# A pre-norm's per-token scale behind the projection, in a two-layer hybrid decoder trunk on one core

## The reference, cut to what matters

```
x = x + rms_post(Mix(rms_pre(x)))
x = x + rms_post2(ConvFFN(rms_pre2(x)))

def rms_norm(x, w):
    y = x * rsqrt(mean(x * x, axis=-1, keepdims=True) + EPS)
    return y * w
```

## Time and profile before

| | us |
|---|---|
| median of 3 runs | 2903.79 (2901.67 to 2905.25) |
| span of the profiled execution, first to last instruction | 2897.5 |
| the profiled execution's own time | not listed; its span is 6.3 below the median |
| TensorE busy in the span | 2551.8 |
| VectorE busy | 1373.6 |
| ScalarE busy | 961.6 |
| POOL busy | 230.7 |

### The profile page before, as it was taken

How to read it: one execution, slowest core, us unless ns; L and a number is a source line. 1 busy time by engine, 2 the same in 40 slices (tenths; PEclk the granted TensorE clock), 3 DMA queues, 4 the chain that set the end, 5 groups by cost and what they waited for, 6 DMA issues and landing times. The chain is left out here.

```text
span 2897.5 us, 41258 instructions
## 1 busy us (share of the span) xinstructions
PE 2551.8 (88%) x16456; PEld 2166.6 (75%) x16456; DVE 1373.6 (47%) x2125; ACT 961.6 (33%) x1396; POOL 230.7 (8%) x350
## 2 busy tenths in 40 slices
PE   6999487998999889999888995879989997999996
PEld 6658333766999879999885782346679997999895
DVE  3338454356333366663342475433563334666623
ACT  3122523332222345553230224332322223454521
POOL 0014132002000000000000132210020000000000
PEclk9999668667999999999999995776779999999998
DMA  3462100221222212222315420012212222222221
GB/s 148 121 192 77 37 1 25 66 66 59 88 88 88 80 52 95 89 95 81 108 59 159 147 73 26 1 42 70 63 62 88 88 80 66 74 95 88 89 88 59
DMA packets 84178, 229.90 MB, mean 79 GB/s; under 512 B 10386, under 2 KB 27794, under 8 KB 83090
## 3 DMA queue, kind: packets, MB, share of 16 engines
q1 hardware_dynamic: 71426, 204.16, 22.0%
q10 hardware_dynamic: 12560, 23.11, 2.5%
HBM read 216.68 MB, written 10.55 MB: 78 GB/s over the span
## 5 line engine op out<-in xcount | busy, mean ns | idle before, releaser
L439 PE MATMUL PS<-XH,WH 128*128 128x260 f32 x3616 | 749.5, 289 | 59.6 <-DVE XL L1195 34.9
L439 PE MATMUL PS<-XL,WH 128*128 128x260 f32 x3616 | 734.5, 285 | 4.1 <-issue 2.7
L439 PE MATMUL PS<-XH,WL 128*128 128x260 f32 x3616 | 733.9, 285 | 0.0
L1219 DVE TENSOR_TENSOR WL<-R,WH 128x1024 fp32r<-128x1024 f32 x240 | 294.3, 1226 | 852.2 <-ACT WH L913 851.8
L913 ACT ACTIVATE WH<-R 128x1024 fp32r<-128x1024 f32 x270 | 285.9, 1059 | 1017.0 <-PE PS L439 860.7
L439 PEld LDWEIGHTS PS<-XH,WH 128*128 128x128 f32 x3616 | 567.5, 191 | 69.7 <-issue 44.8
L439 PEld LDWEIGHTS PS<-XL,WH 128*128 128x128 f32 x3616 | 563.7, 190 | 4.5 <-issue 4.5
L439 PEld LDWEIGHTS PS<-XH,WL 128*128 128x128 f32 x3616 | 563.3, 191 | 0.0
L439 PE MATMUL PS<-FR,WH 128*128 128x260 f32 x1024 | 187.4, 285 | 0.0
L1198 DVE SCALAR_TENSOR_TENSOR S<-S,V 128x510 f32<-128x510 f32 (+1 forms) x176 | 132.1, 751 | 44.9 <-ACT S L1162 41.8
L439 PEld LDWEIGHTS PS<-FR,WH 128*128 128x128 f32 x1024 | 151.0, 190 | 0.1
(11 more groups left out here) (302 smaller groups left out, 3029.8 us busy)
## 6 DMA issues: line engine op xcount, KB each, us to landing
R<-w_up SPq DMA_DIRECT2D x88, 512.0 KB, 3.3
R<-w_gate SPq DMA_DIRECT2D x64, 512.0 KB, 3.3
R<-w_proj SPq DMA_DIRECT2D x58, 512.0 KB, 3.4
R<-v_c SPq DMA_DIRECT2D x128, 192.0 KB, 2.4
R<-w_down SPq DMA_DIRECT2D x44, 512.0 KB, 3.3
R<-k_c SPq DMA_DIRECT2D x72, 256.0 KB, 3.2
R<-k_c ACTq DMA_DIRECT2D x56, 256.0 KB, 3.6
R<-w_br SPq DMA_DIRECT2D x16, 512.0 KB, 3.3
```

The source lines that it names most:

```text
L439: i = mm(PS[:, bank + a, 0:HALF], p[:, w, k * 128:(k + 1) * 128], x[:, a * HALF:(a + 1) * HALF], start=first and p is WH and x is hi, stop ...
L1219: v_.tensor_tensor(WL[:, half(l, m), :], slot(l, SPLIT[m]), WH[:, half(l, m), :].bitcast(f32), ALU.subtract).then_inc(w_lo.sem, 1)
```

## The change

A token's scale RB no longer goes into the projection's input. `XH` and `XL` are now the parts of X x weight alone, and each tile is multiplied by RB when it leaves PSUM: by VectorE for projection tiles 0 to 11, the gates and the up-projection (`proj_out`, `g_raw`, `up_raw`); for projection tiles 12 to 28 ScalarE copies as before and POOL multiplies in place (`scale_projection`). ScalarE's sigmoid and the up-projection's first convolution tap then read the scaled tile from SBUF. The gates' splits of weights run two tiles ahead to the end, so that the out-projection's first two are among them.

Tiles 0 and 1 of each of the four projections behind a pre-norm run together (`first_pair`): per chunk 12 products for both and the sum of the squares. They wait for that chunk's `XL` alone, which VectorE makes between the residual's updates, one chunk behind (`xl_part`); the reciprocal comes after them (`norm_scale`).

At the start the vectors come first, x comes in four pieces of two chunks, the constants in two, with the first two weight tiles in between, and each engine waits for what it uses. y leaves in four pieces, each as soon as its two chunks are updated. The constants' columns are reordered so that the identity, the ones and EPS come first.

```
--- before.py
+++ after.py
...
+        def proj_bank_free(l, c):
+
+            return proj_out.nth(l, c) if c < CUT else proj_raw.nth(l, c - CUT)
...
-            for dst, src in ((X[:, :, :], x_in), (K[:, :], consts), (V[:, :, :], vecs)):
-                sp.dma_start(dst, src).then_inc(loaded.sem, 16)
-            sp.wait_ge(pt_loaded.sem, 16)
+            sp.dma_start(V[:, :, :], vecs).then_inc(v_loaded.sem, 16)
+
+            def load_x(i):
+                sp.dma_start(X[:, 2 * i:2 * i + 2, :], x_in[:, 2 * i:2 * i + 2, :]).then_inc(x_loaded[i].sem, 16)
...
             for l in range(L):
+                if l == 0:
+                    load_x(0)
                 for c in range(CUT):
                     tile(l, proj(c), w_proj[l, c], 1024)
+                    if l == 0 and c == 0:
+                        sp.dma_start(K[:, 0:C_EARLY], consts[:, 0:C_EARLY]).then_inc(early.sem, 16)
+                    if l == 0 and c == 1:
+                        for i in range(1, 4):
+                            load_x(i)
+                        sp.dma_start(K[:, C_EARLY:NC_], consts[:, C_EARLY:NC_]).then_inc(loaded.sem, 16)
+                        sp.wait_ge(pt_loaded.sem, 16)
...
-            sp.wait_ge(norm_out.sem, L * norm_out.per)
-            sp.dma_start(y_out, X[:, :, :]).then_inc(stored.sem, 16)
+            for i in range(4):
+                sp.wait_ge(*x_new.nth(L - 1, 8 + 2 * i + 1))
+                sp.dma_start(y_out[:, 2 * i:2 * i + 2, :], X[:, 2 * i:2 * i + 2, :]).then_inc(stored.sem, 16)
...
-            pe.wait_ge(loaded.sem, 48)
+            pe.wait_ge(early.sem, 16)
...
+            def first_pair(l, half_, n0, n1):
+
+                for n in (n0, n1):
+                    pe.wait_ge(*w_hi.nth(l, split_no[n]))
+                    pe.wait_ge(*lo_ready(l, split_no[n]))
+                for k in range(KD):
+                    pe.wait_ge(*xl_ready.nth(l, 8 * half_ + k))
+                    for i, n in enumerate((n0, n1)):
+                        ins = block_split(half(l, split_no[n]), k, XH[:, k, :], XL[:, k, :], 2 * i, k == 0, k == KD - 1)
+                        if k == KD - 1:
+                            ins.then_inc(tile_used.sem, 1)
+                    pe.wait_ge(*sq_ready.nth(l, 16 * half_ + k))
+                    for a in range(2):
+                        ins = mm(PS[:, 4 + a, 0:HALF], kc(C_ONE), S[:, k % 2, a * HALF:(a + 1) * HALF],
+                                 start=k == 0, stop=k == KD - 1)
+                    ins.then_inc(sq_summed.sem, 1)
...
-                norm_sum_chunks(l, 0)
+                first_pair(l, 0, proj(0), proj(1))
+                if l == 0:
+                    pe.wait_ge(loaded.sem, 16)
 
                 def project(c):
-                    if c >= 2:
-                        pe.wait_ge(*proj_out.nth(l, c - 2))
-                    dense_split(l, proj(c), 2 * (c % 2), x_parts, *[normed(l, 0)] * (c == 0))
+                    pe.wait_ge(*proj_bank_free(l, c - 2))
+                    dense_split(l, proj(c), 2 * (c % 2), x_parts)
...
-                            pe.wait_ge(*g_sig.nth(l, q - 2))
+                            pe.wait_ge(*g_raw.nth(l, q - 2))
                         dense_split(l, nb - 4 + br, 2 * (q % 2), x_parts, *[again] * (q == 0))
...
-                norm_sum_chunks(l, 2)
-
-                for j in range(2 * JF):
+                first_pair(l, 1, FIRST["up"], FIRST["up"] + 1)
+
+                for j in range(2, 2 * JF):
+                    if j == 2:
+                        pe.wait_ge(*root_ready.nth(l, 2))
                     if j >= 4:
-                        pe.wait_ge(*up_evac.nth(l, j - 4))
-                    dense_split(l, FIRST["up"] + j, 2 * (j % 4), x_parts, *[normed(l, 2)] * (j == 0))
+                        pe.wait_ge(*up_raw.nth(l, j - 4))
+                    dense_split(l, FIRST["up"] + j, 2 * (j % 4), x_parts)
...
+            act.wait_ge(v_loaded.sem, 16)
+            act.wait_ge(early.sem, 16)
             act.wait_ge(pt_loaded.sem, 16)
 
-            def squares(l, j, before):
+            def pre_norm(l, half_, col, ready):
+
                 for k in range(KD):
-                    before(k)
+                    ready(k)
+                    do(A(XH[:, k, :], X[:, k, :], ACT.Identity, scale=V[:, l, col + k:col + k + 1]), xh_ready)
+                    if l == 0 and half_ == 0 and k == 1:
+                        split(0, 0)
+                        split(0, 1)
                     if k >= 2:
-                        act.wait_ge(*sq_summed.nth(l, 8 * (j // 2) + k - 2))
+                        act.wait_ge(*sq_summed.nth(l, 8 * half_ + k - 2))
                     do(A(S[:, k % 2, :], X[:, k, :], ACT.Square), sq_ready)
+                root(l, 2 * half_)
...
+                pre_norm(l, 0, V_NPRE, (lambda k: act.wait_ge(*x_new.nth(l - 1, 8 + k))) if l else
+                         (lambda k: act.wait_ge(x_loaded[k // 2].sem, 16)))
...
                 for c in range(NPROJ):
                     act.wait_ge(*tile_done(l, proj(c)))
                     if c + 2 < NPROJ and c + 2 not in (CUT, CUT + 1):
                         split(l, c + 2)
-                    do(A(halves(F[:, c, :]), pair(2 * (c % 2)), ACT.Copy), proj_out)
+                    if c >= CUT:
+                        do(A(halves(F[:, c, :]), pair(2 * (c % 2)), ACT.Copy), proj_raw)
...
                 for q in range(32):
                     act.wait_ge(*tile_done(l, FIRST["gate"] + 5 * (q // 4) + q % 4))
-                    if q + 2 < 32:
-                        split(l, NPROJ + q + 2)
-                    if q >= 4:
-                        act.wait_ge(*br_used.nth(l, q - 4))
-                    do(A(halves(S[:, q % 4, :]), pair(2 * (q % 2)), ACT.Sigmoid), g_sig)
+                    split(l, NPROJ + q + 2)
+                    act.wait_ge(*g_raw.nth(l, q))
+                    do(A(S[:, q % 4, :], S[:, q % 4, :], ACT.Sigmoid), g_sig)
                     if q % 4 == 1 and q > 4:
                         merged_leading(q // 4 - 1)
-                split(l, S_OUT)
-                split(l, S_OUT + 1)
                 merged_leading(KD - 1)
...
-                squares(l, 2, lambda k: act.wait_ge(*norm_out.nth(l, 8 + k)))
-                root(l, 2)
-                leading(l, 1)
+                pre_norm(l, 1, V_FPRE, lambda k: act.wait_ge(*x_new.nth(l, k)))
...
                         ch = g * JF + j
                         act.wait_ge(*tile_done(l, FIRST["up"] + m))
                         split(l, S_UP + m + 2)
-                        if m >= 2:
-                            act.wait_ge(*fcv.nth(l, m - 2))
-                        else:
-                            act.wait_ge(*norm_out.nth(l, 23))
-                        do(A(halves(S[:, g, :]), pair(2 * (m % 4)), ACT.Copy))
+                        act.wait_ge(*up_raw.nth(l, m))
                         do(A(FO[:, ch, :], S[:, g, NPR - 2:TOK], ACT.Copy))
                         if j:
                             act.wait_ge(*h_ready.nth(l, j - 1))
-                        do(A(halves(S[:, 2 + g, :]), pair(2 * (m % 4)), ACT.Identity,
+                        do(A(S[:, 2 + g, :], S[:, g, :], ACT.Identity,
                              bias=V[:, l, V_FCB + ch:V_FCB + ch + 1],
                              scale=V[:, l, V_FCW + 3 * ch + 2:V_FCW + 3 * ch + 3]), up_evac)
...
-            def pre_norm(l, j, col):
-                dve.wait_ge(*root_ready.nth(l, j))
-                do(v_.reciprocal(RB[:, :], S[:, 3, :]))
-
-                def rest(k):
-                    dve.wait_ge(*xh_ready.nth(l, 4 * j + k))
-                    tt(XL[:, k, :], S[:, k % 2, :], XH[:, k, :].bitcast(f32), ALU.subtract, norm_out)
-                for k in range(KD):
-                    if k >= 2:
-                        rest(k - 2)
-                    stt(S[:, k % 2, :], X[:, k, :], V[:, l, col + k:col + k + 1], RB[:, :], ALU.mult, ALU.mult,
-                        xt_ready)
-                rest(6)
-                rest(7)
+            def xl_part(l, half_, col, k):
+                dve.wait_ge(*xh_ready.nth(l, 8 * half_ + k))
+                stt(XL[:, k, :], X[:, k, :], V[:, l, col + k:col + k + 1], XH[:, k, :].bitcast(f32), ALU.mult,
+                    ALU.subtract, xl_ready)
+
+            def norm_scale(l, half_):
+                dve.wait_ge(*root_ready.nth(l, 2 * half_))
+                do(v_.reciprocal(RB[:, :], S[:, 3, :]), rb_ready)
...
                 for k in range(KD):
                     stt(S[:, 4, :], F[:, out + k, :], V[:, l, col + k:col + k + 1], S[:, 3, :], ALU.mult, ALU.mult)
-                    tt(X[:, k, :], X[:, k, :], S[:, 4, :], ALU.add, norm_out)
+                    tt(X[:, k, :], X[:, k, :], S[:, 4, :], ALU.add, x_new)
+                    if k and j == 1:
+                        xl_part(l, 1, V_FPRE, k - 1)
+                    elif k and l + 1 < L:
+                        xl_part(l + 1, 0, V_NPRE, k - 1)
+                if j == 1:
```

(55 more changed lines are left out.)

68 lines of the change are left out of this document (29 added, 39 removed).

## The result

The changed kernel takes 2867.7 us, the median of four runs (2859.0 to 2876.4), against 2904.5 before: 0.9878 of it, interval 0.9856 to 0.9900. The forecast was 2879.8. So the direction was right, and the time lies 4.3 us outside the range on the fast side. The profiled run has a span of 2859.9 us and a time of 2861.6; its span is 37.6 shorter than that of before.

What follows compares the result with a forecast made beforehand. With TensorE busy 88% of the span, the prediction targeted places where the chain leaves it, such as pre-norms. Terms 12.6 + 5.1 + 3.3 + 1.0 + 3.4 - 1.4 = 24.0 us saved gave 2879.8 us, range 2872 to 2893.

Steps and rivals of the forecast that it cites:

- 1.4 lost: At the transposes, POOL's scaling of the keys slows VectorE's convolution sums: 0.7 us per layer, bounds 0 and 3.2.
- The pairs: Tiles 0 and 1 run along with the residual's update at three pre-norms: 4.2 us saved each, 12.6 in all.
- The start: Needed loads land earlier, TensorE starts at 13.6 us; the first pair and wait end at 44.5 against 49.6: 5.1 saved.
- Gates: Gates to out-projection: earlier weight splits end TensorE's 1.65 us idle in each layer: 3.3 saved, 0 if it merely moves.
- end of the up stage: ScalarE's first copy leaves the chain at the up stage's end: 0.5 us per layer, 1.0 saved.
- output: The last quarter of y lands 3.3 us after its issue, where the span ended 6.75 after: 3.4 saved.
- Covers: VectorE's scalings at the gates and inside the up stage fit beside other work and cost nothing; uncovered, the gates' add 45 us.
- Rival (b): POOL's scalings hold VectorE's top-k during projections 12 to 28, and so TensorE: slower, 2923.6 us; chance 0.04.
- The second pass of rest parts: At the gates, removing RB from POOL's and VectorE's second pass is hidden, since the first gate tile's chunks come in time.
- (a): The pairs give nothing: new wait, cold starts and slow sums eat the gain; 2897.5 us, chance 0.08.
- (c): The clock does not rise within the pair: 16.4 us more, four times; 2945 us, chance 0.02.
- (d): No change: the new order doesn't run along, VectorE takes 3.5 us a chunk, not 2.32; 2903.0 us, chance 0.05.

Runs made afterwards that it cites:

- the quiet POOL: Changed kernel with POOL scaling the keys tile by tile during the projection, so nothing on POOL meets the first convolution sum: 2879.25 us, 0.9922 of before.
- the fillers: Products nobody reads, put on TensorE ahead of the recurrence stage and in its first wait: 2868.0 us on the changed kernel, 2849.9 on the fastest version.

## Why the prediction was right and wrong, point by point

**The step that failed** is the loss of "1.4 lost" for POOL and VectorE at the transposes, and the sum that stopped there. Its size was right: 0.75 a layer, on the very operations named. But it was entered as the end of a chain. What stands behind it, a stage of 110 to 119 us whose length hangs on when it starts, had no term, no bound and no rival; the trace of before had it at 0.76 of the clock, and I read the clock only around the pre-norms. In the profiled run the 0.75 us put that stage where it takes 110 us, and 1.5 lost went with 15.7 gained; in the second profile of the same kernel the stage gave 5.0. With the loss taken away (the quiet POOL) the stage gained nothing in the profile, and the kernel takes 2879.25 us. The forecast was 2879.8 us; that it meets this so closely is luck, since the other terms were off by 3.2 in sum. Chance has a part in the measured time too: of the nine runs of the changed kernel three lie inside the forecast's range, at 2873.5 to 2876.4.

**From span to median.** The forecast carried over 6.3 us between the profiled span of before and the median. The runs listed since stand only 1.7 to 2.1 above their own spans, so most of the 6.3 was a profiled run that was faster than the median. It did no harm: the profiled span of after stands 7.8 below its median.

**The pairs.** Pair 20.3 to 21.3 us (forecast 21.0), idle behind three of them 6.43 (6.3) and at the start 7.71 (7.6 with the table load), then a restart at half clock for 3.6 to 5.1 us (4.6). In the up stages 5.8 and 4.5 saved, against 4.2: the mechanism and the size hold. Ahead of layer 1's projection the table has 1.6 in place of 4.2. The pair itself gave 2.4: from the post-norm's sum to the end of the projection's ninth tile it took 84.5 us in before and 82.1 in after, and the same to 0.1 in six more profiles whose edits do not reach it. The remaining 0.8 was lost behind that, in the stretch discussed under the start. At this pair the clock fell as the post-norm's own sum began, which took 2.05 us instead of 1.14, and the pair ran at 0.50 for its first 5.5 us, where the up stage's pair of layer 1 did so for 3.4. This term was mis-sized by the clock: one price was given to three places.

**The start.** TensorE's first product came at 15.84 instead of 13.6. ScalarE had to load its table first, 1.28 us, which the sum counted for the root only, and began at 8.46 (forecast 7.7) when the first constants landed. In the kernel before the same load ran early, under the wait for x; so the change itself put it on the path (timelines, before and after):

```profile
2.11 1.28 ACT L903 ACT_TABLE_LOAD   x1 [2.11 <-DMA PT<-pages]
```

```profile
8.46 1.28 ACT L938 ACT_TABLE_LOAD   x1 [8.46 <-DMA K<-consts]
```

The rest of the sequence held; 3.4 saved in place of 5.1. Of the 3.4, 2.9 were there when the ninth tile was done. The stretch from there to the transposes, in either layer, took 211.1 to 216.0 us over eight profiles whose edits do not reach it, with 4.7 to 8.9 us in which TensorE waited for loads of the cached keys. So a few us between two profiles, or two totals, come from there without any cause in the kernel.

**Gates, end of the up stage, output.** 3.26 of 3.3, 0.89 of 1.0, 2.8 of 3.4: right, the first shown alone.

**Covers.** The scalings at the gates and in the steady up stage cost nothing, as said. Rival (b), POOL's scalings holding the top-k, had no part: MAX8 takes 1217 ns as before.

```profile
L1345 DVE MAX8 M<-T 8x8 f32<-8x1025 f32 x64 | 77.9, 1217 | 19.3 <-ACT T L988 17.2
```

The second pass of rest parts, entered as hidden, gave 0.6 a layer ahead of the first gate tile; which of its two shorter halves, POOL's or VectorE's, was not tried.

**Rivals.** (a), (c) and (d) had no part: the pairs behind a post-norm gave 12 us, the clock rose within each of them, and a chunk takes what was forecast on VectorE (2419.74 to 2422.07 from rest part to rest part, 2.33).

## What to carry to other kernels

Sum a forecast over all stages, those that the change does not touch too: where TensorE works between waits and its granted clock goes up and down, a stage's length can hang on its start, and a shift of less than 1 us ahead of it can be worth ten times as much, with either sign. Put that spread into the range; and where a change or a variant moves such a stage, compare the stages, not the totals, and those of more than one profile, before anything is said about the change itself.

When a serial tail (root, reciprocal, read-out) stands behind a burst of products, put the preparation of the next product ahead of it on every engine and give that product a place that needs no read-out. Here that was worth more than the wait alone, 6 to 9 us a place, since the clock did not fall.

## What the runs showed of the hardware that I had not expected

One stage, with the same instructions on all engines, took 109.9 to 118.9 us, in steps rather than evenly, by where it met the rise of TensorE's clock. Work added ahead of it made the kernel before faster, by 6.5 and 7.5 us in the medians for 2.5 and 1.7 us put in, and 1.5 us of contention taken away made the changed kernel 14 us slower. The Trainium skill (TensorE: Matmul & The Clock Gate, Part 1) says that the gate does not start anew with a kernel, so that the place of a change of level varies. The runs agree as far as they go: two profiles of the changed kernel, unedited, have the first rise 18.0 and 17.9 us behind the starts of their stages in the one, and 17.8 and 18.5 in the other. What decides a rise or a fall inside the stage stays open, and so does why the fillers ahead of it raised the clock only for a time.
